# An expert's gate weights in four pieces, and two fetches moved ahead of another on one DMA queue

## The reference

```python
w = jax.nn.softmax(top_v, -1) * p_group
expert = g_top[:, None].astype(jnp.int32) * EXPERTS_PER_GROUP + top_i
...
hb = jax.nn.silu(xb @ w_gate[e]) * (xb @ w_up[e])
return hb @ w_down[e]
```

## Time and profile before

| | |
|---|---|
| median of 3 runs | 915.26 us (913.98 to 917.81) |
| the profiled execution | 915.11 us |
| its span, first to last instruction | 913.3 us |
| PE, DVE, ACT, POOL busy | 94%, 43%, 21%, 22% of the span |
| moved by DMA | 242.19 MB, mean 265 GB/s |

### The profile page before, as it was taken

How to read it: one execution, slowest core, us unless ns; L and a number is a source line. 1 busy time by engine, 2 the same in 40 slices (tenths; PEclk the granted TensorE clock), 3 DMA queues, 4 the chain that set the end, 5 groups by cost and what they waited for, 6 DMA issues and landing times.

```text
span 913.3 us, 15676 instructions
## 1 busy us (share of the span) xinstructions
PE 859.7 (94%) x5478; PEld 531.6 (58%) x5478; DVE 388.5 (43%) x1009; ACT 194.0 (21%) x452; POOL 202.7 (22%) x293
## 2 busy tenths in 40 slices
PE   8999999999999999999989999998999989887985
PEld 3444876557888888845655555554555544444432
DVE  4991584876465564615871222221222211111117
ACT  1320338762212121201111111110111101010121
POOL 3010014666001010100042333321332223122212
PEclk9999999999999999999999999998999999999989
DMA  9261881008622220595569999999999999999955
GB/s 327 78 95 69 131 74 70 1 5 327 246 92 93 70 93 24 191 408 213 205 223 418 420 419 419 422 422 425 421 422 423 420 420 421 423 424 422 420 187 227
DMA packets 44660, 242.19 MB, mean 265 GB/s; under 512 B 14895, under 2 KB 15503, under 8 KB 28196
## 3 DMA queue, kind: packets, MB, share of 16 engines
q1 hardware_dynamic: 32646, 230.70, 65.2%
q0 software_dynamic: 10096, 9.65, 4.1%
q10 hardware_dynamic: 1872, 1.24, 0.8%
HBM read 244.43 MB, written 21.30 MB: 291 GB/s over the span
## 4 chain that ended last, share of the span: by engine, by line
PE 65%; SPq 16%; DMA 10%; DVE 5%; issue 3%; ACT 1%; POOLq 0%; POOL 0%; DVEq 0%; ACTq 0%
PE ps L770 18%; SPq L398 11%; PE ps L923 11%; PE ps L538 6%; PE ps L819 6%; PE ps L953 6%; DMA arena<-experts 4%; DMA reg_a<-experts 4%; SPq L395 4%; PE ps L530 3%; PE ps L682 2%; PE ps L704 2%; PE ps L726 2%; PE ps L600 2%; PE ps L914 1%
## 5 line engine op out<-in xcount | busy, mean ns | idle before, releaser
L923 PE MATMUL ps<-arena,reg_a 128*64 128x256 f32 x1024 | 123.9, 394 | 16.1 <-DMA arena<-experts 14.3
L923 PEld LDWEIGHTS ps<-arena,reg_a 128*64 128x64 f32 x1024 | 74.9, 141 | 62.0 <-issue 29.3
L2042 POOL DMA_INDIRECT ye_scratch<-reg_bo,reg_u x62 | 62.3, 1004 | 184.6 <-ACT reg_bo L1240 144.5
L1840 DVE TENSOR_TENSOR small<-reg_u,ps 128x128 f32<-128x128 f32 x62 | 17.8, 288 | 194.4 <-ACT reg_u L1233 176.7
L1847 DVE COPY small<-ps 128x128 f32<-128x128 f32 x62 | 18.1, 292 | 116.6 <-PE ps L943 116.6
L1233 ACT ACTIVATE reg_u<-ps 128x128 f32<-128x128 f32 x62 | 17.2, 278 | 225.6 <-PE ps L923 225.6
L1240 ACT COPY reg_bo<-ps 128x512 f32<-128x512 f32 x62 | 36.4, 586 | 134.3 <-PE ps L953 82.2
L953 PE MATMUL ps<-arena,small 128*64 128x512 f32 x256 | 61.2, 599 | 0.9 <-DVE small L1847 0.9
L538 PE MATMUL ps<-xT,reg_bo 128*128 128x512 f32 x128 | 55.7, 595 | 0.0
L819 PE MATMUL ps<-reg_a,reg_bo 128*128 128x512 f32 x128 | 55.7, 593 | 0.0
L770 PE MATMUL ps<-xT,arena 128*128 128x256 f32 x224 | 51.0, 379 | 0.0
(11 more groups left out here) (374 smaller groups left out, 1349.9 us busy)
## 6 DMA issues: line engine op xcount, KB each, us to landing
arena<-experts SPq DMA_DIRECT2D x32, 2048.0 KB
arena<-experts SPq DMA_DIRECT2D x32, 1024.0 KB
reg_a<-experts SPq DMA_DIRECT2D x7, 2048.0 KB
x<-experts SPq DMA_DIRECT2D x6, 2048.0 KB, 35.9
reg_bo<-experts SPq DMA_DIRECT2D x6, 2048.0 KB
xT<-experts SPq DMA_DIRECT2D x5, 2048.0 KB
arena<-mid_w SPq DMA_DIRECT2D x8, 1024.0 KB, 4.9
reg_bo<-experts SPq DMA_DIRECT2D x7, 1024.0 KB
```

The source lines that it names most:

```text
L923: m = pe.matmul(ps[2 + c % 2][64 * h:64 * h + 64, 0:DE], xgT[:, x, BLK * (c % 2):BLK * (c % 2 + 1)], gates[k][:, x * 512 + h * DE:x * 512 ...
L2042: pool.indirect_dma_start(ye_dram, bass.IndirectOffsetOnAxis(scol[k], 0), yb[k], None, bounds_check=4 * L - 1, oob_is_err=False).then_inc( ...
```

## The change

Two edits, both in the program of SP, with three semaphore increments on PE. The gate part of slot 6 is fetched as four transfers of 512 KB, one per token tile of `x1`: the first three wait for `s_womm` at 9, 10 and 11, which `first_tokens(0)` to `first_tokens(2)` now raise, the fourth for `s_xt` as before. Then the fetches of positions 8 and 9 (slots 0 and 1, gate and down) are all issued before slot 7's down part, which waits for `s_idx`; before, slot 0's gate part alone stood ahead of it. The positions from 10 on follow as they did.

```diff
-        FIRST_PARTS = [1, 1, 1, 1, TT, 1, 1, 2]
+        FIRST_PARTS = [1, 1, 1, 1, TT, 1, TT, 2]
...
             sp_.wait_ge(s_x1d, 16 * TT)
-            sp_.wait_ge(s_xt, 1)
-            gate_part(6, 6)
+            for t in range(TT):
+                if t < TT - 1:
+                    sp_.wait_ge(s_womm, 2 * TT + t + 1)
+                else:
+                    sp_.wait_ge(s_xt, 1)
+                sp_.dma_start(gates[6][:, t * D:(t + 1) * D], a["experts"][rows_of(6), t * D:(t + 1) * D]).then_inc(s_wg[6], 16)
...
                 e = row_of(FORCED)
                 sp_.wait_ge(s_gu, 1)
                 gate_part(e, 0)
+                with sp_.If(extra > 1):
+                    e1 = row_of(FORCED + 1)
+                    sp_.wait_ge(s_gu, 2)
+                    gate_part(e1, 1)
+                sp_.wait_ge(s_dn, 1)
+                down_part(e, 0)
+                with sp_.If(extra > 1):
+                    sp_.wait_ge(s_dn, 2)
+                    down_part(row_of(FORCED + 1), 1)
             sp_.wait_ge(s_idx, 2)
             down_part(7, 7)
-            with sp_.If(extra > 0):
-                e = row_of(FORCED)
-                sp_.wait_ge(s_dn, 1)
-                down_part(e, 0)
-                for j in range(1, UN):
-                    with sp_.If(extra > j):
-                        expert(row_of(FORCED + j), j, j + 1)
+            for j in range(2, UN):
+                with sp_.If(extra > j):
+                    expert(row_of(FORCED + j), j, j + 1)
...
-            first_tokens(0)
+            first_tokens(0).then_inc(s_womm, 1)
...
-            first_tokens(1)
+            first_tokens(1).then_inc(s_womm, 1)
...
-            first_tokens(2)
+            first_tokens(2).then_inc(s_womm, 1)
```

## The result

The changed kernel takes 917.44 us (median of 20 runs, 916.22 to 919.3); the kernel before, 913.93 us over 20 runs (912.16 to 918.47). The ratio of the runs is 1.0027, with an interval of [1.0017, 1.0038]; the quotient of the two medians is 1.0038, at the upper edge (four of the 20 runs before lie at 917.8 to 918.5). So the change makes the kernel slower by about a quarter of a per cent, where 912.2 us and 0.34% faster were forecast. It lies within the 0.5% that I counted as no change and outside the range of 909.3 to 915.6, on the wrong side. The profiled execution after has a span of 915.7 us against 913.3.

A forecast was written before the change was run, and what follows sets the result against it. The prediction took the gapless DMA fetch stream from 480 us on as the bound. Four pieces 0 and reordered fetches -3.1 us turned 915.1 into 912.0, or 912.2 against the median; 8-in-10 range 909.3 to 915.6.

The forecast's parts named there:

- The bound, the three holes and the worth of a gap: DMA stream sets the end from 480 us; holes at 458-462, 468-470, 476-481; each idle microsecond removed saves one.
- Part one at 0: Gate part 6 in four pieces only moves idle time around 458 to 464 us: 0, bounds 0 to 0.7 us saved.
- The queue's order and times: SP's queue: gate 9 at 471.3, down 8 at 475.2, down 9 at 477.8, down 7 by 478.7; 476-481 hole filled, 3.07 us.
- who waits for what moved later: After the reorder: down 7 has 26 us slack; second gather loses up to 5.1 us, covered; gate 10 stays at 484.4.
- Rival 2: Lead lost again, hole reappearing at gate 10 or 601 to 617 us, or old order no obstacle: 915.1 us, chance 0.17.
- The end: Expert phase's end: stream stays gapless, so the last gate wait comes 3 us earlier than 871.5.

The follow-up runs named there:

- e1: Kernel before with only slot 6's gate part fetched in four pieces, old fetch order kept; 914.02 us, ratio 0.9986 [0.9972, 1.0001].
- e2: Changed kernel with slot 6's gate part fetched whole, so only the new fetch order remains; 917.41 us, ratio to before 1.0032.
- e3: Changed kernel with slot 1's new gate part sent only after the first gather has landed; 915.37 us, ratio to before 0.9996.
- e8: Changed kernel with position 8's down part sent before position 9's gate part, which waits for the first gather's landing; 915.43 us, ratio to before 1.0017.
- e12: Kernel before plus 44 small idle products on PE ahead of its wait for the first gather; 917.79 us, ratio to before 1.0042.
- e9: Changed kernel with slot 1's early gate part in 4 KB rows and 17 idle products ahead of PE's gather wait; 915.38 us, ratio to before 1.0001.
- e5: Changed kernel with slot 1's early gate part sent as four transfers of 4 KB rows instead of 16 KB rows; 915.28 us, ratio to before 1.0022.
- e6: Changed kernel with slot 1's early gate part sent as two transfers of 8 KB rows; 916.06 us, ratio to before 1.0024.
- e10: Changed kernel with the gate parts of slots 0 and 1 both in 4 KB rows; 917.63 us in one run.
- e11: Changed kernel with 2 MB more queued behind slot 1's gate part, a copy to a scratch tensor in memory; 925.53 us in one run.
- e7: Changed kernel plus 20 small idle products on PE ahead of its wait for the first gather; 918.40 us, ratio to before 1.0055.

## Why the prediction was wrong

*The bound, the three holes and the worth of a gap* held in the main. Over 440 to 500 us the kernel before moved 17.8 MB (60 x 296 GB/s) and the changed one 16.7 (60 x 279); the missing 1.0 MB at 421 GB/s is 2.4 us. Over 500 to 520 us it moved 408 GB/s against 424, another 0.8 us. So its stream is some 3.2 us behind, and its span is 2.4 us longer. That the first sum alone also gives 2.4 is chance: e1's stream lacks as much over 440 to 500 us (279 GB/s, with a list 2.6 us later), and its span of 914.0 us is only 0.7 longer. What the end adds is told below.

*Part one at 0* held (e1). Piece 0 left at 455.25 and not at 453.4, since the write-back of x1 landed later than 453; the queue ran empty at about 465 and not at 463.5. Neither cost anything that e1 shows. The 2.0 us for each transfer that the prediction names from the Trainium skill ("DMA: Bandwidth & Descriptors", Anatomy of one DMA) are stated there for transfers issued by GpSimd, and these pieces are issued by SP.

*The queue's order and times* held to within 0.6 us up to down 7, and the hole of 476 to 481 was filled (428 GB/s against 421 forecast).

*The step that failed is "who waits for what moved later".* It set the gather's loss at 5.1 us at most and called it covered, because gate 10 would cost only when more than 3.6 us late; but 5.1 is more than 3.6, so by its own numbers the cover was short. Three more things were wrong in it. First, it looked at the second gather, issued at 476.74, whose tokens PE turns only at 489.90. The turn at 478.06, ahead of slot 2's product, waits for the first one, issued at 474.47, and gate 9's early fetch, out at 472.02, now runs beside it. Second, the row behind the 5.1, the landing times of 2.6, 3.2 and 7.7 us over all transfers of this tensor, does not stand for gathers beside a full stream: the view of DMA issues gave no landing time for them at all, so the 3.2 can only be of plain transfers (the write-back of x1 stands at 2.9 there). It did have one for indirect transfers of POOL beside the stream, the 62 scatters into `ye_scratch`, at a median of 7.9 us. The trace after has 9.2 to 11.1 us for the gathers from 520 us on, median 10.0:

```profile
DMA to landing us min/median/max: 9.2/10.0/11.1
```

Third, the step summed the gather alone. It left out that PE, once it stands for 6 us, goes on at half clock and needs 2.3 us more for the turn and slot 2's product. So gate 10 was 8.56 us late, not 3.6 or less. Rival 2 named this very mechanism ("at gate 10, if gathers make PE over 3.6 us late") and priced it at 915.1, no gain; it took its worst to be the loss of the lead, and did not ask how long the new hole could be. It is longer than the old one: 490 to 496 misses (421 - 109) x 6 = 1.9 MB or 4.4 us, against the 3.07 that the early fetches gain. The 1.4 us between them, 0.7 from the later list and the 0.8 missing over 500 to 520 us come near the 3.2 us by which the stream is behind.

*The end* did not go as the prediction had it, with the last gate wait 3 us before 871.5. In the changed kernel PE's last wait for a fetch ends at 860.00 and is for an earlier position's; behind it PE works to the end of the list without standing for another:

```profile
819.60 40.28 DMA arena<-experts
...
860.00 3.68 PE L933 MATMUL ps<-arena,reg_a 128*64 128x256 f32 x16 [3.89 <-DMA arena<-experts]
```

The chain still goes back to a fetch of 40.3 us, as the bound needs, but the clock has a share in the end too. Sixteen products take 1.95 us at full clock and 3.68 here, behind 3.89 us of standing; before they take 3.11 behind the wait at 871.48, and in e1 1.95. So the span of one profiled execution carries a microsecond or two that the stream does not explain.

What is shown: the loss comes from part two (e1, e2); it goes through the gather that shares the engines with the early fetches (e3, e8), and a late PE with a late gate 10 is enough for such a loss (e12, without any early fetch). That it is gate 10 and not PE's own lateness is argued from the drained queue, not tested apart. The small differences between the versions do not follow gate 10's time: e9, at 22.0 us from gate 8, stands at 1.0001, and e8, at 20.6, at 1.0017. What stays open: why a gather beside a full queue takes 9 to 11 us and how that divides between the rows' length and the bytes queued ahead (e5, e6, e9, e10 and e11 lie between the theories), and what the clock is worth by itself. No version tried beats the kernel before; e1 and e3 have ratios below 1, neither clear of 1.

## What to carry to other kernels

A quiet stretch of the DMA engines is not free to fill when a small transfer on the critical path runs in it: look up who else uses the engines there, and what its landing time is under load, before you count the gap as gain. When a view gives one range over several kinds of transfers, find out which kinds it has measured. And price a delay by what follows it in a chain (the wait, the clock behind the wait, the fetches that hang on the work), to the next point where the stream can run dry.

## What the runs showed of the hardware

A gather of 128 rows of 4 KB, issued by GpSimd, was followed by its user after 3.6 us beside a draining queue, after 6.4 us with 1 MB issued 0.7 us behind it, and after 7.2 to 10.5 us with the full queue of the changed order. In e8 the gather was issued first and was late all the same.

The tensor engine's clock fell to its lower level in the stretch behind the wait: granted 0.50 over 484 to 490 us after 6.04 us of idleness. It fell in e8 after 3.16 us idle, a turn at full clock and 1.43 us idle, when the 48 products took 8.36 us in place of 5.40, and in e9 after 1.86 us, a turn and 1.43 us. In the kernel before it stayed up there after 0.39 and 1.43 us.

It also fell in the router's stage of six of the profiled executions (e1, e3, e7, e10, e11, e12; granted 0.79 over 462 to 470 us), of kernels with old and new order alike: slot 0's 32 products took 5.3 us in place of 3.67 there, and gate 8 went out about 2 us later. In e1:

```profile
462.00:470.00 8.00, 6.30 (x42) 4.44 (x42) 7.45 (x35) 0.56 (x1) 5.60 (x10) 0.79 0.35 132
```

The one profile of the kernel before does not have it (granted 1.00 there), so whether it is a part of that kernel's own scatter of 912 to 918 us is not shown.
